# Spreading the input projection over the heads of an attention stage: fourteen pieces in a head instead of fifteen, twelve in the last instead of six

## What is computed

```
mod = SiLU(c) @ w_ada + b_ada                       -> shift, scale, gate (twice)
h = x * (1 + scale1) + shift1
[q | k | v | u | gate logits] = h @ w_in            one projection, for prompt and sample
branch A: causal pooling on u, a linear map         (1024 channels, 128 for each head's turn)
branch B: differential attention, 8 heads: rotary on q and k,
          softmax(q1 k1) - lambda * softmax(q2 k2), times v, RMSNorm of each head
merged = sigmoid(g_pool) * A + sigmoid(g_attn) * B
x = LN(alpha * x + (1 + gate1) * merged @ w_out)
x = LN(alpha * x + (1 + gate2) * HierMoE(x * (1 + scale2) + shift2))
```

## Time and profile before

| | |
|---|---|
| three runs | 1608.69 us median (1607.84 to 1611.46) |
| the profiled execution | 1608.85 us, span 1607.0 us |
| PE matmuls | 1357.8 us busy (84%), 7980 instructions |
| PE weight loads | 1146.5 us (71%) |
| DVE | 992.0 us (62%) |
| ACT | 703.5 us (44%) |
| POOL | 273.8 us (17%) |
| mean granted clock of PE | 0.917 |
| the attention stage | ends near 1003 us; head 6 runs from 802.02 to 893.76 us, head 7 follows |

### The profile page before, as it was taken

The page is one execution under the profiler, slowest core; times in us unless marked ns, Lnnn a source line. Parts: engine busy times, 40 slices in busy tenths (PEclk is TensorE's granted clock), DMA queues, the critical chain, the costliest instruction groups (busy, mean ns, idle before and its releaser), DMA issues.

```text
span 1607.0 us, 23013 instructions
## 1 busy us (share of the span) xinstructions
PE 1357.8 (84%) x7980; PEld 1146.5 (71%) x7980; DVE 992.0 (62%) x1500; ACT 703.5 (44%) x1185; POOL 273.8 (17%) x145
## 2 busy tenths in 40 slices
PE   7799787999999999999999785689729999999900
PEld 3467386989898988989899584468527887788700
DVE  2332314758667575757657562555566998999769
ACT  1212212445454353535445442311016988898712
POOL 1400011111111111111111000154321111112050
PEclk9899998999999999999999886779858999999955
DMA  9643623323223332323223110934109889565494
GB/s 313 194 143 130 207 81 85 93 66 94 80 80 93 84 104 83 92 66 95 87 80 93 53 53 19 306 126 143 70 1 327 293 300 384 205 213 200 144 287 147
DMA packets 211355, 229.42 MB, mean 143 GB/s; under 512 B 18070, under 2 KB 185178, under 8 KB 211131
## 3 DMA queue, kind: packets, MB, share of 16 engines
q1 hardware_dynamic: 196011, 173.52, 34.3%
q0 software_dynamic: 6976, 25.23, 4.8%
q10 hardware_dynamic: 8280, 29.51, 4.7%
HBM read 173.20 MB, written 46.79 MB: 137 GB/s over the span
## 4 chain that ended last, share of the span: by engine, by line
PE 65%; DVE 15%; DMA 5%; ACT 5%; SPq 4%; issue 4%; POOL 2%; ACTq 0%; DVEq 0%; POOLq 0%
PE S L843 6%; PE S L845 6%; PE S L844 6%; PE T L902 4%; PE T L903 4%; PE T L906 4%; PE PB L902 4%; PE PB L906 3%; PE PB L903 3%; PE S L1007 3%; PE S L858 3%; ACT F L1327 3%; PE PB L858 2%; DVE F L1888 2%; PE T L1033 2%
## 5 line engine op out<-in xcount | busy, mean ns | idle before, releaser
L1327 ACT ACTIVATE R<-F 128x1024 fp32r<-128x1024 f32 (+2 forms) x302 | 292.9, 1016 | 150.9 <-DVE F L1757 46.4
L843 PE MATMUL S<-R 128*128 128x512 f32 (+1 forms) x528 | 213.4, 404 | 35.1 <-POOL R L2277 29.6
L2269 POOL TENSOR_TENSOR R<-F,R 128x1024 fp32r<-128x1024 f32 x40 | 99.3, 2483 | 672.9 <-ACT R L1327 672.9
L844 PE MATMUL S<-R 128*128 128x512 f32 (+1 forms) x528 | 208.9, 396 | 0.0
L845 PE MATMUL S<-R 128*128 128x512 f32 (+1 forms) x528 | 208.7, 395 | 0.0
L902 PE MATMUL PB<-R 128*128 128x344 f32 x480 | 157.9, 333 | 4.2 <-ACT R L1327 3.1
L902 PE MATMUL T<-R 128*128 128x344 f32 x480 | 158.6, 334 | 0.0
L903 PE MATMUL T<-R 128*128 128x344 f32 x480 | 153.0, 322 | 0.0
L903 PE MATMUL PB<-R 128*128 128x344 f32 x480 | 152.1, 320 | 0.0
L843 PEld LDWEIGHTS S<-R 128*128 128x128 f32 (+1 forms) x528 | 99.6, 189 | 61.5 <-issue 36.1
L1327 ACT ACTIVATE R<-T 128x512 fp32r<-128x512 f32 x144 | 82.7, 596 | 116.5 <-PE T L1033 75.8
(11 more groups left out here) (253 smaller groups left out, 2776.4 us busy)
## 6 DMA issues: line engine op xcount, KB each, us to landing
F<-in_w_ada SPq DMA_DIRECT2D x24, 1024.0 KB
F<-in_w_in SPq DMA_DIRECT2D x44, 512.0 KB, 4.0
F<-in_w_e_gate SPq DMA_DIRECT2D x16, 1024.0 KB
F<-in_w_e_up SPq DMA_DIRECT2D x16, 1024.0 KB
F<-in_w_e_down SPq DMA_DIRECT2D x16, 1024.0 KB, 9.0
y_d<-F ACTq DMA_DIRECT2D x32, 512.0 KB
out<-F SPq DMA_DIRECT2D x24, 512.0 KB, 4.6
F<-F SPq DMA_DIRECT2D x192, 43.0 KB, 1.9
```

The costliest lines, as they stand in the source:

```text
L843: mm(out, w[0], m[1], start=start, stop=False)
L844: mm(out, w[1], m[0], start=False, stop=False)
L1327: return nc.scalar.activation(out, in_, func, **kw)
L2269: nc.gpsimd.tensor_tensor(whl[c % 2][1], wraw2[c % 2], whl[c % 2][0].bitcast(F32), ALU.subtract).then_inc(w_lo.sem, 1)
```

## The change

The lists are built from two tables. Heads 0 to 4 and 6 take 14 pieces, head 5 takes 15 and the last head 12. A head of 14 has one piece instead of two in step 1. The order of the pieces stays, so each head of 14 begins one place further back: the last gate pieces of a head are done in the first steps of the next one (one in head 1, five in heads 5 and 6, six in head 7). `step_above` gives the list of the step before, and in the last step's case that of the head before. DVE's rotations, which followed one step behind in steps 1 to 3, and its pool gates, which had places of their own in steps 5 to 7, are now both done from `pieces(h, i)`, in every step, one step behind PE. Where `pieces` stands is in the diff: in step 4 ahead of `weights(h, 2)`, in step 5 ahead of `page_weights(h)`, in step 6 ahead of `weights(h, 4)`, in step 0 ahead of `weights(h - 1, 7)`.

```diff
--- before.py
+++ after.py
@@ -531,12 +531,25 @@
         h, c = chunk_of(g // 3)
         return h, 3 * c + g % 3
 
+    PER_HEAD = (14, 14, 14, 14, 14, 15, 14, 12)
+    PER_STEP = {15: (2, 2, 2, 2, 2, 1, 2, 2), 14: (2, 1, 2, 2, 2, 1, 2, 2), 12: (2, 1, 2, 2, 2, 1, 1, 1)}
+
     def step_pieces(h, i):
 
-        first = 9 + 15 * h
-        if h == H - 1:
-            return [first + j for j in {4: (0,), 5: (1,), 6: (2, 3), 7: (4, 5)}.get(i, ())]
-        return [first + j for j in ((0, 1), (2, 3), (4, 5), (6, 7), (8, 9), (10,), (11, 12), (13, 14))[i]]
+        first = 9 + sum(PER_HEAD[:h]) + sum(PER_STEP[PER_HEAD[h]][:i])
+        return [first + j for j in range(PER_STEP[PER_HEAD[h]][i])]
+
+    def piece_of(h, n):
+
+        return next(g for g in range(3 * N_CHUNKS) if kind(g) == (h, n))
+
+    def step_above(h, i):
+
+        if i:
+            return step_pieces(h, i - 1)
+        return step_pieces(h - 1, 7) if h else []
+
+    assert sum(PER_HEAD) == 3 * N_CHUNKS - 9 and all(sum(PER_HEAD[:h + 1]) >= 9 + 15 * h for h in range(H - 1))
 
     PBANK = (PB, TB[1])
     SQBANK = (Sb[1], Sb[3], TB[0])
@@ -1931,14 +1944,14 @@
         def pool_gate(h, k):
 
             turn = 3 * h + k
-            copied(dve, 9 + 15 * h + (k if h == H - 1 else 9 + k))
+            copied(dve, piece_of(h, 9 + k))
             if k == 0:
                 dve.wait_ge(poolc_landed, (h + 1) * 16)
             cols = slice(k * PIECE, (k + 1) * PIECE)
             STT(out=poolc[:, cols], in0=gate0[turn % 2], scalar=1.0, in1=poolc[:, cols], op0=ALU.add, op1=ALU.mult).then_inc(gate0_used.sem, 1)
 
         def merge(h):
-            copied(dve, 9 + 15 * h + (5 if h == H - 1 else 14))
+            copied(dve, piece_of(h, 14))
             osT_copied.wait(dve, h, 0)
             sq_done.wait(dve, h, 0)
             V(STT(out=O32, in0=gate1, scalar=1.0, in1=O32, op0=ALU.add, op1=ALU.mult))
@@ -1947,10 +1960,13 @@
             gate0_used.wait(dve, h, 2)
             TT(poolc, poolc, O32, ALU.add).then_inc(merged.sem, 1)
 
-        def ropes(h, i):
-            for g in step_pieces(h, i):
-                if kind(g)[1] < 6:
+        def pieces(h, i):
+            for g in step_above(h, i):
+                owner, n = kind(g)
+                if n < 6:
                     rope(g)
+                elif 9 <= n < 12:
+                    pool_gate(owner, n - 9)
 
         for g in range(6):
             rope(g)
@@ -1964,13 +1980,14 @@
                     if h:
                         weights(h - 1, 6)
                     combine(h, i)
+                    pieces(h, 0)
                     if h:
                         weights(h - 1, 7)
                 if i == 1:
                     if h:
                         weights(h - 1, 8)
                     sample_queries(h)
-                    ropes(h, 0)
+                    pieces(h, 1)
                     combine(h, i)
                     if h:
                         weights(h - 1, 9)
@@ -1978,34 +1995,35 @@
                     page_products(h)
                     weights(h, 0)
                     combine(h, i)
-                    ropes(h, 1)
+                    pieces(h, 2)
                     operands_v(h)
                 if i == 3:
                     combine(h, i)
-                    ropes(h, 2)
+                    pieces(h, 3)
                     if h:
                         merge(h - 1)
                 if i == 4:
                     weights(h, 1)
                     combine(h, i)
+                    pieces(h, 4)
                     weights(h, 2)
                     page_scores(h)
                 if i == 5:
                     page_max(h)
                     combine(h, i)
+                    pieces(h, 5)
                     page_weights(h)
-                    pool_gate(h, 0)
                 if i == 6:
                     weights(h, 3)
                     combine(h, i)
+                    pieces(h, 6)
                     weights(h, 4)
-                    pool_gate(h, 1)
                 if i == 7:
                     weights(h, 5)
+                    pieces(h, 7)
                     if h < H - 1:
                         operands_qk(h + 1)
                     combine(h, i)
-                    pool_gate(h, 2)
         for n in range(6, 10):
             weights(H - 1, n)
         merge(H - 1)
```

## The result

| | before | after |
|---|---|---|
| median | 1609.17 us (1607.84 to 1611.46, 4 runs) | 1635.88 us (1634.08 to 1637.7, 4 runs) |
| span of the profiled execution | 1607.0 us | 1634.7 us |
| mean granted clock of PE | 0.917 | 0.915 |

The changed kernel takes 1.0165 times as long, with a 95% interval of 1.0147 to 1.0182: 26.7 us more, where I forecast 18.7 more. The predicted time of 1627.4 us is 8.5 us short; the result lies within the range, and the direction is right.

What follows compares the result with a forecast made beforehand. PE's work bounds seven heads, the score-to-weights chain the last. Pieces -22.4, steps 3 to 6 +31.4, small terms -4.0 + 1.2 + 1.4, last head +8.1, clock +3: +18.7, 1627.4 us; own range 1612 to 1641, overall 1602 to 1645.

Steps and rivals of the forecast that it cites:

- The pieces: Step 1 of six heads loses a piece: 3.7 us off in five heads, 3.9 in head 0, sum -22.4.
- the uncovered wait: Step 1, weights' rest of group 9 on DVE once its covering piece goes: costed at nothing, 0 to 1.2 us each.
- POOL takes its turn at the end of DVE's running operation: POOL's residual stops DVE's operations with two SBUF inputs (rotations, merges, combinations): 2.3 us per new meeting, bounds 0 and 2.4.
- Rival 1: The order costs, but POOL misses DVE's operations in the heads: 1602.7 us, faster; chance 0.14.
- The Trainium skill's rule: Whichever engine starts first keeps an exclusive lock; read strictly, two step 6 waits go, 4.4 us off the sum.
- The rotations in steps 4 to 6: Rotations slip ahead of weights PE awaits: two cost 3.1 us, one 1.6; with POOL, steps 3 to 6 sum +31.4.
- Clock, +3: PE's lower clock behind ten waits of 2 to 4 us: between 0 and 17 us, taken as +3.
- Rival 3: The clock: each of ten waits costs its 1.7 us in full, +14, 1641 us; chance 0.11.
- The last head: Steps 0 to 2 +7.9, steps 3 to 6 +3.5, step 7 -3.3 us: together +8.1.
- The small terms: Head-start waits gone in five heads -4.0; split before k and v copies +1.2; page columns in heads 0, 3 +1.4.
- The signs: PE waits 2 to 4 us in steps 4, 6 of heads 1 to 6; slow operations beside POOL; listed head lengths.
- head 1's chain: Steps 3 to 6: 2.4 + 3.1 = 5.5 late, PE sees 4.6; old 1.08 wait goes, leaving 3.4 us.

Runs made afterwards that it cites:

- Experiment 5: Changed kernel with POOL's rest of raw weights cut to 8 of 1024 columns in three of 40 chunks (step 1 of heads 0, 3, 7): 1625.87 us, ratio 1.0099.
- experiment 6: Kernel before, with POOL's rest of raw weights written as four operations of a quarter each: 1598.05 us, ratio 0.9943.

## Why the prediction was right, and where it was short

- **The pieces.** Step 1 takes 8.76 to 8.78 us in heads 1, 2, 4 and 6, against 12.39: 3.6 each, where I had 3.7. What failed is the clause "I cost the uncovered wait at nothing (0 to 1.2 us for each)". I looked at DVE's rotations as what could hold up group 9, and not at where POOL's operation falls in that step, nor at the combination ahead of group 9, which waits for turn 9. In heads 3 and 7 it measured 2.0 of wait and 1.5 of clock, in head 0 as much in another place. Experiment 5 prices the three at 10.9 us by the heads' lengths, and 10.0 by the medians; my sum was 8.5 short. That the rest nearly adds up is in part luck, as the next points show.
- **POOL takes its turn at the end of DVE's running operation.** Right, and the largest part: all the meetings that I had counted off ACT's order took place (the merge of heads 1 and 3 at 3.3 us, the rotation of heads 2 and 6 at 2.7, of heads 4 and 5 at 2.6, the combination of head 6 at 3.35, the page columns of heads 0 and 3 at 2.32). Rival 1, that POOL misses, is out: the meetings are in the rows, and with POOL short the change costs 2.7 us, not 26.7.
- **The Trainium skill's rule** (SBUF — State Buffer, SBUF: two separate sides), that whichever starts first keeps the lock for its whole instruction: by it, read strictly, 4.4 us would have come off. The trace doesn't agree with that part: at 888.42 DVE is listed 0.03 us ahead of POOL and is the one that waits, as it was before. It does agree with the whole instruction as the unit: one operation of DVE lost 2.2 us to the whole and 0.53 to a quarter.
- **The rotations in steps 4 to 6.** The heads' changes from 4 to 6 came out at +0.9, +4.6 and +4.3 for +1.0, +5.1 and +3.6, but two errors cancel. In step 4 and at the page scores head 4 loses 1.03 us (0.68 + 0.35), about the 1.2 I gave it; at group 4 PE waits 3.66. Together 4.7, where the old 1.08 and my shift of 5.5 make 6.6. The difference is the clock: without waits that step takes 11.99 us (experiment 6), with 3.66 of wait that is 15.65, and it took 17.32 at a granted clock of 0.90. So the shift was over by 1.9 and the clock, under its own heading, was under by 1.7.
- **Clock, +3.** Too small, and the step of the sum that was furthest off beside the one above. By the same subtraction step 6 of heads 4, 5 and 6 lost 1.7, 1.7 and 2.0 us to it, and step 2 of heads 0, 3 and 7 lost 1.7, 1.5 and 1.5, at mean granted clocks of 0.86 to 0.90: 10 us. Step 7 of head 2 lost 1.5 more; it has no wait in it and took 14.78 us before, at 1.00:

```profile
511.00:527.32 16.32, 16.32 (x109) 13.96 (x107) 9.00 (x14) 5.62 (x11) 0.00 (x0) 0.90 0.09 27
```

  Nor did the clause "Most are followed by another wait on DVE, which swallows the loss" hold: behind the waits of 3.55 and 2.84 us in step 4 of heads 2 and 6, step 5 ran at 0.76 and 0.82 and took 7.24 and 6.86 us instead of 5.80, without a wait. In step 4 of heads 1 and 3 there was nothing to swallow, for the waits of 1.54 to 1.66 us left the clock at 1.00. Rival 3 had much of the truth, then, and its 1641 us is nearer to 1635.88 than my 1627.4; but it priced all ten waits alike, and heads 1 and 3 speak against that.
- **The last head.** +8.1 forecast, +13.0 measured. The merge late by the piece and POOL, and the gate in step 4 late by the reload (DVE waits 1.15 us for it at 968.72, I had 1.4) are there. 3.6 of the missing 4.9 are the meeting of step 1. Steps 3 to 6 took 42.18 us, where I had 42.1. Another 1.1 stands in step 7, to the tail's first turn: 13.21 us instead of the 12.1 of my terms, at a granted clock of 0.87 behind a wait of 3.11 us.
- **The small terms.** The wait of 0.80 at a head's start went in heads 1, 2, 4, 5 and 6 as forecast. The split ahead of the copies of k and v cost less than I had: where PE turns the sample's rows of k and v, 0.25 us of waiting became 0.40 in heads 2, 5 and 6, so 0.15 each instead of 0.4. The page columns cost 1.16 of waiting and 1.4 of step length in each of heads 0 and 3 (16.16 us for step 7 instead of 14.79), where I took 1.4 for both: the upper bound of 1.5 each was the right end.
- **The signs.** I had said 2 to 4 us for each wait in steps 4 and 6 of heads 1 to 6. Four of them are (3.55, 3.66, 3.65 and 2.84), ten are 0.67 to 1.84, and head 1 has none in step 6. Heads 2, 4, 5 and 6 came within 1.4 us of the lengths I gave; head 3 (97.67 for about 93) and the last (92.39 for 87 or 88) did not. In head 1's chain 5.5 less 1.0 is 4.5, which I wrote as 4.6; the 3.4 that it gives is right.

## What to carry to other kernels

Where one engine's operation stops another engine's, list for every step which operation of the one stands at the moment when the other becomes ready, and do it again for the steps in which a cover is removed, not only where work is added; three of the costliest meetings here were with a 0.48 us operation. Cutting the blocking operation into quarters costs only busy time that nobody waits for (POOL 302 to 308 us instead of 273) and pays where one operation waits behind it, while a row of operations that it can stop pays most of the whole in instalments.

Before moving work to fill another stage's gaps, put what nobody waits for behind what somebody waits for, and count what slips with it. With POOL short, the heads in which two and three rotations had slipped into steps 4 to 6 (1 and 2) kept 2.5 and 2.0 us of their piece, and those with four or five (3, 4 and 6) kept nothing. A wait can also cost twice, once itself and once by the lower clock behind it.

## What the runs showed of the hardware that I had not expected

- An operation of almost no length can be held as long as a large one. The page columns' last operation is 8x8 elements and took 2.32 us beside POOL in the changed kernel's head 0 (0.22 without). It reads one input from SBUF and a scalar from PSUM, so "two SBUF inputs" is not the whole of what POOL stops. In the kernel before, the 128x1 operation shown above took 2.14 us instead of 0.16, in six heads.

```profile
327.58 2.32 DVE L1942 TENSOR_SCALAR sm<-cst,T 8x8 f32<-8x8 f32 x1
```

- Behind a wait of 2.00 us of PE the granted clock was 0.57 over the 4 us from 552.00, where the 1.08 us waits of before left it at 1.00. The length of the wait alone doesn't tell: behind 1.33 us in head 2 it was 0.69 over the 4 us from 510.00, and behind the waits of 1.54 to 1.66 us in heads 1 and 3 it stayed at 1.00.
- POOL's quarters are slowed too: four take 3.98 and 4.21 us beside DVE in the rows above, and 2.8 where DVE leaves them alone, against 2.39 for the whole.
